# Local attention taken out of the recurrent chain and set among the gb projections, with ga projections in single contraction steps in its place

## The reference, cut to what matters

```python
proj = h @ w_in
aq, ak, av, bq, bk, bv, bz, ba, bb, ga, gb = jnp.split(proj, ...)
ya = swa_sink_attention(aq, ak, av, sink, rel_bias)     # 8 heads of 64, window of 128 keys, softmax with a sink
yb = gated_deltanet(bq, bk, bv, bz, ba, bb, ...)        # 4 heads of 128, chunkwise recurrence
merged = sigmoid(ga) * (ya @ w_up_a) + sigmoid(gb) * (yb @ w_up_b)
x = x + merged @ w_out
```

## Time and profile before

| | |
|---|---|
| time, median of 3 runs | 911.11 us (910.9 to 918.97) |
| the profiled execution: time, span | 917.6 us, 915.7 us |
| PE busy | 791.2 us, 86% of the span |
| DVE, ACT, POOL busy | 356.3, 244.5, 305.0 us |
| granted PE clock, mean | 0.942 |

### The profile page before, as it was taken

How to read it: one execution, slowest core, us unless ns; L and a number is a source line. 1 busy time by engine, 2 the same in 40 slices (tenths; PEclk the granted TensorE clock), 3 DMA queues, 4 the chain that set the end, 5 groups by cost and what they waited for, 6 DMA issues and landing times.

```text
span 915.7 us, 15044 instructions
## 1 busy us (share of the span) xinstructions
PE 791.2 (86%) x5907; PEld 659.2 (72%) x5907; DVE 356.3 (39%) x766; ACT 244.5 (27%) x421; POOL 305.0 (33%) x264
## 2 busy tenths in 40 slices
PE   5999999979988899998999898974999999887830
PEld 5888898868876788786799777863777767664620
DVE  6378750763567324233610712352111221111127
ACT  4333232431341234402222644330111111101003
POOL 3723344422250316213443344232333333322102
PEclk9999999999999889999999998976999999999985
DMA  9745504312021202464467273563999999999933
GB/s 252 132 96 102 115 2 92 65 29 46 1 47 47 47 1 48 96 188 97 96 189 161 47 230 132 213 242 136 390 392 387 395 388 387 382 385 391 369 137 162
DMA packets 73563, 162.88 MB, mean 178 GB/s; under 512 B 18876, under 2 KB 48396, under 8 KB 65320
## 3 DMA queue, kind: packets, MB, share of 16 engines
q1 hardware_dynamic: 65968, 150.66, 51.9%
q0 software_dynamic: 5696, 10.50, 3.3%
q10 hardware_dynamic: 1848, 1.02, 0.7%
HBM read 157.57 MB, written 13.04 MB: 186 GB/s over the span
## 4 chain that ended last, share of the span: by engine, by line
PE 63%; DMA 11%; DVE 11%; issue 7%; ACT 4%; POOL 2%; SPq 1%; DVEq 0%; POOLq 0%; ACTq 0%
PE bank L966 14%; PE bank L973 10%; PE bank L1295 10%; PE bank L974 10%; PE bank L975 10%; PE bank L1305 5%; DMA ring<-in_w_exp_down 4%; DMA arena<-in_w_exp_down 4%; PE bank L1282 2%; DMA ring<-in_w_cq 1%; DMA ring<-in_w_up_a 1%; DVE xres L1937 1%; PE bank L1316 1%; ACT w_high L1349 1%; DVE rt L1914 1%
## 5 line engine op out<-in xcount | busy, mean ns | idle before, releaser
L973 PE MATMUL bank<-h_hi,w_high 128*128 128x512 f32 x296 | 120.1, 406 | 0.0
L974 PE MATMUL bank<-h_lo,w_high 128*128 128x512 f32 x296 | 118.5, 400 | 0.0
L1295 PEld LDWEIGHTS bank<-arena,hT 128*64 128x64 f32 x1728 | 98.9, 138 | 24.7 <-issue 23.4
L789 POOL TENSOR_TENSOR ring_low<-ring,w_high 128x2048 fp32r<-128x2048 f32 (+1 forms) x16 | 72.3, 4522 | 114.3 <-ACT w_high L1349 114.1
L1295 PE MATMUL bank<-arena,hT 128*64 128x128 f32 x1728 | 102.5, 277 | 8.0 <-DMA arena<-in_w_exp_down 7.2
L789 POOL TENSOR_TENSOR w_low<-ring,w_high 128x2048 fp32r<-128x2048 f32 x14 | 64.4, 4598 | 80.8 <-ACT w_high L1349 80.7
L1910 DVE SCALAR_TENSOR_TENSOR rt<-rt,bank 128x128 f32<-128x128 f32 x32 | 9.2, 288 | 185.5 <-ACT rt L1550 185.5
L1349 ACT ACTIVATE w_high<-ring 128x2048 fp32r<-128x2048 f32 (+1 forms) x32 | 58.7, 1835 | 71.7 <-PE bank L975 25.7
L973 PE MATMUL bank<-w_high,h_hi 128*128 128x256 f32 (+1 forms) x208 | 63.9, 307 | 4.0 <-ACT w_high L1349 2.2
L975 PE MATMUL bank<-h_hi,ring_low 128*128 128x512 f32 x168 | 67.0, 399 | 0.0
L973 PEld LDWEIGHTS bank<-h_hi,w_high 128*128 128x128 f32 x296 | 56.7, 192 | 13.1 <-issue 0.3
(11 more groups left out here) (273 smaller groups left out, 1427.1 us busy)
## 6 DMA issues: line engine op xcount, KB each, us to landing
arena<-in_w_exp_gate SPq DMA_DIRECT2D x27, 1024.0 KB
arena<-in_w_exp_up SPq DMA_DIRECT2D x27, 1024.0 KB
arena<-in_w_exp_down SPq DMA_DIRECT2D x27, 1024.0 KB
ring<-in_w_in SPq DMA_DIRECT2D x33, 512.0 KB, 6.6
ring<-in_w_exp_gate SPq DMA_DIRECT2D x5, 1024.0 KB
ring<-in_w_exp_up SPq DMA_DIRECT2D x5, 1024.0 KB
ring<-in_w_exp_down SPq DMA_DIRECT2D x5, 1024.0 KB
xres<-in_x SPq DMA_DIRECT2D x8, 512.0 KB, 7.4
```

The source lines that it names most:

```text
L789: after(pool.tensor_tensor(low, full, high, ALU.subtract), w_lo)
L973: pe.matmul(o, l_hi, r_hi, start=(n == 0), stop=False)
L974: pe.matmul(o, l_hi, r_lo, start=False, stop=False)
L1295: ins = pe.matmul(bank[CAP * half:CAP * half + CAP, 1, P * n:P * n + P], xgT[:, x, kk, :], w[:, kk, P * half:P * half + P], start=(kk == 0 ...
```

## The change

- `sc`, `pt` and `pv` leave the chain. They stand behind it, among the eight gb jobs, with ty 0 to 3 in one place behind gb:2. The scores of even and odd tiles have a buffer each (in `xres`), and so have `stat` and `sums`.
- A ga job is cut into 8 contraction steps: seven new jobs `gp` and the last one, still called `ga`, all eight summed in one bank that is theirs alone while they last. The chain has the other 7 in turn. `pieces_after` says how many of them follow a job of the chain (0, 1 or 2).
- The output norm is made once for all four chunks, at gb:1, by DVE alone. The outputs of all four chunks are kept (`o_sb`), so no chunk waits for an earlier norm.
- The split weights use both halves of `w_high` in turn for all chunks, also those of the gates. The places at which POOL makes the softmax product are fixed (`SOFTMAX_AT`).
- The memory rows are loaded into `hT` and not into `rows`, after the last o2. The residual rows `x` are loaded again at the third up-projection chunk and not at the first.
- cv:0 and cv:1 are now halves of the columns, one chunk each, and not halves of the rows with two chunks each. The four ub of a half come ahead of the four ua. The split of yaT moves from gb:1 to cv:0, that of ybT stays at gb:4.

```diff
+def pieces_after(job):
+    k = job[0]
+    if k in ("tA", "tk", "tAT", "tv"):
+        return 1
+    if k in ("P", "PX") and job[1] % 2:
+        return 1 if job[2] < 5 else 2
+    return 2 if k in ("u", "S") or job == ("w", 1) else 0
...
-    for k, job in enumerate(delta):
+    pieces = [("gp", f, kk) if kk < KD - 1 else ("ga", f) for f in range(8) for kk in range(KD)]
+    for job in delta:
         jobs.append(job)
-        while n < len(other) and n * len(delta) < (k + AHEAD) * len(other):
-            jobs += other[n]
-            n += 1
-    jobs += [("gb", f) for f in range(3)] + [("ty", 2), ("ty", 3)] + [("gb", f) for f in range(3, 8)]
+        for _ in range(pieces_after(job)):
+            jobs += pieces[:1]
+            pieces = pieces[1:]
+    jobs += pieces
+    sc = [[("sc", t, 0), ("sc", t, 2), ("sc", t, 1), ("sc", t, 3)] for t in range(NT)]
+    pt = [[("pt", t, g) for g in range(4 if t else 2)] for t in range(NT)]
+    jobs += sc[0] + [("gb", 0)] + sc[1] + [("gb", 1), ("gb", 2)] + [("ty", c) for c in range(NT)] + pt[0] + sc[2] + [("gb", 3), ("pv", 0)]
+    jobs += pt[1] + sc[3] + [("gb", 4), ("pv", 1)] + pt[2] + [("gb", 5), ("pv", 2)] + pt[3] + [("gb", 6), ("pv", 3), ("gb", 7)]
...
-        jobs += [(k, f) for k in ("ua", "ub") for f in range(4 * half, 4 * half + 4)]
+        jobs += [(k, f) for k in ("ub", "ua") for f in range(4 * half, 4 * half + 4)]
...
-SOFTMAX_LEAD, NORM_LEAD = 3, 3
+SOFTMAX_AT = {("gb", 1): 0, ("sc", 2, 0): 1, ("sc", 3, 0): 2, ("gb", 5): 3}
...
     if k == "cv":
-        return [("cv", 0), ("cv", 256)]
+        return [("cv", 256 * job[1])]
...
+    for n, job in enumerate(jobs):
+        gates = at["gp", 0, 0] <= n <= at["ga", 7]
+        if job[0] in ("gp", "ga"):
+            bank_index[job] = BANKS - 1
+        else:
+            turn_no = (turn_no + 1) % (BANKS - 1 if gates else BANKS)
+            bank_index[job] = turn_no
...
+                if k in ("gp", "ga"):
+                    kk = job[2] if k == "gp" else KD - 1
+                    return split_sums(o, [(w_parts(c0, kk, P * (job[1] % 2), P), h_parts(kk))], KD, kk)
...
+                if job == ("gb", 1):
+                    job_empty(dve, ("o2", NT - 1))
+                    dve.wait_ge(zs_ready, 4)
...
+                    for ch, h in itertools.product(range(NT), range(B_HEADS)):
+                        n = 4 * ch + h
+                        ins = stt(out=zs[:, ch, h], in0=o_sb[ch][:, h], scalar=o_scale[:, n:n + 1], in1=zs[:, ch, h], op0=ALU.mult, op1=ALU.mult)
+                        mark(ins) if h < 3 else after(ins, y_ready)
```

More of the change, by code:

```diff
@@ L200, in emptied_by @@
 def emptied_by(job):
+    if job[0] == "gp":
+        return None
     return "act" if job[0] in ON_ACT or job[:2] == ("hT", "ffn") else "dve"
@@ L254, in program @@
                 xsum_count[summed] = count = count + 1
-    softmax_at = {jobs[at[("pt", t, 0)] - SOFTMAX_LEAD]: t for t in range(NT)}
-    norm_at = {jobs[at[("ty", c)] - NORM_LEAD]: c for c in (0, 2)}
     chunks, last_use = [], {}
@@ L281, in program, with before_part @@
         split_at[said.get(c) or first_use[split_chunks[m - 1]]] = m
-    high_of, before_in = [], []
-    for m, c in enumerate(split_chunks):
-        gate = c[0] == "w_in" and C_GA < c[1] <= C_GB
-        high_of.append(high_of[-1] if gate else 1 - high_of[-1] if m else 0)
-        earlier = [n for n in range(m) if high_of[n] == high_of[m]]
-        before_in.append(earlier[-1] if earlier else None)
-    assert high_of[part_of["w_in", C_GA]] == 1
+    def before_part(m):
+        return split_chunks[m - 2] if m >= 2 else None
+    bank_index, before_in_bank, held, turn_no = {}, {}, {}, 0
+    for n, job in enumerate(jobs):
[5 more added lines that the diff above has]
+            bank_index[job] = turn_no
+        before_in_bank[job] = held.get(bank_index[job])
+        held[bank_index[job]] = job
     bias_rows = nc.dram_tensor("bias_rows", (A_HEADS, WIN, BIAS_W), F32, kind="Internal").ap()
@@ L313, in program @@
         ids = sb("ids", [P, 2 * NT], I32)
[L314 removed]
+        TINY = 984
         tiny = sb("tiny", [P, TINY])
@@ L365, in program @@
         work["p"] = work["e"]
+        o_sb += [work["bgk"][:, b] for b in range(2)]
         ab_part = gate_a[:, 6, :]
@@ L577, in bank_of @@
         def bank_of(job):
-            return bank[:, at[job] % BANKS, :]
+            return bank[:, bank_index[job], :]
         def columns(tile, n, odd):
@@ L1200, in emit @@
                 if k == "cv":
-                    m = job[1]
                     job_empty(pe, ("hT", "mem", NM - 1, 1))
-                    for i, c in enumerate(chunks_of(job)):
-                        ins = sums(o[:, 256 * i:256 * i + 256], [(memT[:, kk, m * P:(m + 1) * P], wide(c)[:, kk, :]) for kk in range(KD)])
+                    for m in range(NM):
+                        ins = sums(o[:, 256 * m:256 * m + 256], [(memT[:, kk, m * P:(m + 1) * P], wide(c0)[:, kk, :]) for kk in range(KD)])
                     return ins
@@ L1267, in _ @@
             for n, job in enumerate(jobs):
-                if n >= BANKS:
-                    job_empty(pe, jobs[n - BANKS])
+                if before_in_bank[job] and before_in_bank[job][0] != "gp":
+                    job_empty(pe, before_in_bank[job])
                 if job[0] == "sc" and job[2] < 2:
@@ L1272, in _ @@
                 emit(job if job[0] != "sc" else ("sc", job[1], job[2] - 2)).then_inc(done, 1)
-            for job in jobs[-BANKS:]:
+            for job in held.values():
                 job_empty(pe, job)
@@ L1390, in norm_rows @@
                         job_done(act, ("hT", phase, t - 2, 1))
-                    after(nc.scalar.activation(rows[:, t % 2, :], source(t), ACT.Copy, scale=rstd[:, base + t:base + t + 1]), rows_ready)
+                    dst = rows[:, t % 2, :] if phase != "mem" else source(t)
+                    after(nc.scalar.activation(dst, source(t), ACT.Copy, scale=rstd[:, base + t:base + t + 1]), rows_ready)
                     if phase != "mem" and t >= 2:
@@ L1411, in _ @@
                     act.wait_ge(o_raw, c + 1)
-                    if c == 2:
-                        act.wait_ge(o_ready, 1)
                     for h in range(B_HEADS):
-                        n = 4 * (c % 2) + h
-                        after(nc.scalar.activation(oh4[:, h], o_sb[:, c % 2, h], ACT.Square, accum_out=o_stat[:, n:n + 1]), e if h == 3 else step["act"])
+                        n = 4 * c + h
+                        after(nc.scalar.activation(oh4[:, h], o_sb[c][:, h], ACT.Square, accum_out=o_stat[:, n:n + 1]), e if h == 3 else step["act"])
                 if k == "bias":
@@ L1818, in _ @@
                         rms(NORM_TILES["x"] + 2, 2, rstd_ready)
[L1819 to L1821 removed]
+                if job in (("gb", 4), ("cv", 0)):
+                    n, y = (0, yaT) if k == "cv" else (1, ybT)
+                    dve.wait_ge(h_hi_ready["y"], 2 - n)
                     after(tt(y_lo[:, 4 * n:4 * n + 4, :], y, y_hi[:, 4 * n:4 * n + 4, :].bitcast(F32), ALU.subtract), h_lo_ready["y"])
```

140 lines of the change are left out of this document (57 added, 83 removed).

## The result

The changed kernel takes 899.88 us (median of 4 runs, 899.58 to 899.97). The kernel before took 913.84 us (median of 4 runs, 910.9 to 918.97, the three shown above among them). The ratio is 0.9856, 95% interval 0.9815 to 0.9896. The change gains 14 us, about 1.5%. I had forecast 30 us and a time of 881, so it is faster, as the interval shows, but by less than half of what I said, and the time is outside my range (871 to 896).

The account below looks back on a forecast made before the run. PE was taken as the bound: 229 us = 190 work + 19 idle + 10 clock + about 10 left over. Gains of 25.5 and 5.2, about 30.5, gave 881 us from the median 911.11 (30 applied); range 871 to 896.

Parts of the forecast that it names:

- What bounds the kernel: PE from first G to last memory-row transpose: 229 us = 190 work, 19 idle, 10 clock, about 10 left over.
- 39 us beyond work: PE's idle, half-clock and leftover time in that stretch; 13.5 would be kept and 25.5 gained.
- changes of shape: PE switching between products of different shape: the leftover 10 us, some 40 changes before, about 12 after, 2.5 us kept.
- Part 2: Attention among the gb projections, output norm made once and hidden behind PE's work; gb stage about 75 us.
- pt 3 and pv 2: Gb stage, last softmax tile: pt 3 about 1.1 us late, pv 2 0.8, behind ACT and DVE work; sum 1.9.
- Part 1: Chain without sc, pt, pv and with ga by contraction steps: 7.4 us idle kept, chain about 128 us.
- for chunk b DVE ends some 0.2 us late: Inversion levels in the chain: PE waits 0.2 us for DVE in each of 8 levels, 1.6 us.
- Part 3: cv by column halves, ub ahead of ua: first chunk free 6.9 us earlier, wait and clock loss gone, gain 5.2 us.
- Rival 1: Attention becomes its own chain: each of four tiles delays pt or pv 2 to 3 us; 889 to 893; chance 0.18.
- Rival 4: Waits only move, since GpSimd's splits bound both; gain only 10 to 15 us: 898; chance 0.09.
- Rival 3: Chain recurrence paced by latency, not PE, so slower than before: 931 us; chance 0.05.
- Rival 2: Clock does not hold in the chain: 15 us lost instead of 1.7, 894 us; chance 0.10.

Follow-up runs that it names:

- e3: Changed kernel with the splits of the second and third gb weight chunks moved to o1:3 and pt 0,1: 894.17 us (0.9781).
- e1: Changed kernel with only the split of the second gb weight chunk moved, to o1:3 instead of gb:0: 896.11 us (0.9814).
- e5: Changed kernel with the split of ybT on ACT and DVE at gb:7 instead of gb:4: 904.58 us (0.991).
- e8: Changed kernel with the output norm's 16 DVE products given back to GpSimd as 8 operations: 899.75 us (0.9884).
- e9: Changed kernel with the ga pieces in the chain given out eight at a time, at the same mean rate: 924.31 us (1.0136).
- e11: Changed kernel with two weight splits and ybT split moved, attention one gate later, more setup pieces, memory-row norm at gb:6 instead of gb:5: 888.89 us (0.9742).
- e4: Changed kernel with cv:0 and cv:1 as row halves again, each reading both cv chunks: 905.08 us (0.9907).
- e12: e3 with four GpSimd products that nothing reads added behind the softmax product of tile 0: 899.94 us (0.9843).

## Why the prediction was wrong, step by step

**What bounds the kernel** held: the waits of the earlier trace rows and the falls of the clock beside them could be had. Of the 39 us beyond work I kept 13.5; the kernel kept about 30. One reading was short: a fourth stretch at half clock stands in the chain of before, behind a wait for L849, 3.4 us long (2 x 0.34 x 5):

```profile
270.00:275.00 5.00, 4.16 (x22) 3.79 (x22) 0.69 (x1) 0.46 (x1) 4.92 (x2) 0.66 0.00 0
```

So about 12 of the 39 us are clock, and 8 and not 10 were left for changes of shape; the sum stays.

**The step that failed is in Part 2**: the norm "ready at about 22.5 us after the chain's end, while PE reaches the last ty at 23.2: hidden, with under 1 us to spare". The norm was done after 30.4 us, 9.6 of them in the three meetings, and PE waited 5.1 us for it. In e3, where only the smallest meeting is left, it is done after 22.5; without that one it would be 20.8, an estimate from these numbers. So I had not counted DVE's own work too short (the 16 products take 4.7 us and not my 5.5), and what was missing is that these DVE operations, with both inputs in SBUF, do not run beside a GpSimd product here. The cover was short as well: in e3 PE starts the last ty 22.7 us after the chain's end, 1.4 us of that waiting in ty, and not at 23.2. So even there 1.1 us of waits for the norm is left. I had written that each microsecond beyond the cover is one of PE's, and had not asked which row speaks for a delay. The row at 346.11 did, and so did the mean of 909 ns of that line in the table of groups, beside 160 to 170 ns of its neighbours.

The gb stage, 12.6 us over my 75, in terms:

| term | forecast | measured |
|---|---|---|
| ty behind the norm | 0 | 5.1 |
| gb:2 behind its weights | 0 | 1.8 |
| pt 3 and pv 2 | 1.9 | 2.7 + 0.4 |
| clock | 0 | 14 us at half, some 2 of them idle: 6 |
| work and changes of shape | 73.1 | 87.6 less 10.0 and 6: 71.6 |

The gb:2 wait is a step that I left out: ACT's copy of that chunk stands behind the exponentials of tile 0, and GpSimd's difference starts only at 301.84. That is a queue and no meeting. One entry, in e1, took away this wait and the meeting at L1742. For pt 3 the queue that I counted was the right one, and 1.1 us became 2.7 because y_lo met a difference too: it started at 350.85 and lasted 4.31 us, for 2.29 in e5 where it meets none. The clock is the largest term that I had at nothing. I allowed one fall, for the chain; there was one, at 167.6. The three others stand beside the waits just named, so they are the price of the same errors. A wait of that size does not always bring one: in the profiled executions of e1 and e8 the same wait of 2.0 us stands at the start of the chain, and the clock is 1.00 from 157 to 172 us, where the changed kernel has 0.89. The work was, if anything, less than I said.

**Part 1**: 132.1 us for 128. The waits are 5.0 us, I had 7.4; the clock is as I said. The 6.5 that are left are mostly not idle in the profile. In one level of the inversion:

```profile
193.05 2.27 PE L969 MATMUL bank<-xres 128*128 128x128 f32 x16
```

Two P jobs by the earlier trace rows are 1.78 us; the second waits inside this group for DVE's transpose, which ends at 194.05. A level takes 5.3 us and not 4.9, eight times: 3 us. My "for chunk b DVE ends some 0.2 us late" was too small, the rest (about 3) I cannot place. That single contraction steps hold the chain together was right and undervalued: e9 gives them 23 us.

**How much of the miss is explained.** The time is 18.9 us above the forecast. e3, with two meetings and the gb:2 wait moved away, gives back 5.7, with new meetings in their place; e11, with other places besides and two pieces more in each setup, 11.0. About 8 are left. In e11's profiled execution the chain takes 129.8 us and the gb stage 77.3, together 4.1 over the forecast; for the rest no run here names the cause.

**Part 3** was right in mechanism and size: 5.0 for 5.2, and e4 gives back 5.2 us with the same wait.

**The rivals.** Rival 1, attention as a chain of its own with waits at each tile, is nearest in place and in kind, but its time, 889 to 893, was still too low; it named ACT's queue, and only 4.9 of the 10.0 us are of that kind. Rival 4 had the size (898) with a reason that is half right: "the waits only move, since something else bounds both (GpSimd's splits)". I dismissed it by GpSimd's busy share, which is no evidence when the question is at which moment it is busy. Rival 3's slower ending needs the coarse grain of e9. Rival 2 did not come in the chain.

**The median.** 911.11 was a low draw of the kernel before; 913.84 with one more run. It moves the forecast by 2 to 3 us and doesn't rescue it.

## What to carry to other kernels

When work is moved between DVE and GpSimd, or beside it, count their operations together wherever both read from SBUF, and lay the two timelines over each other before trusting "hidden". A margin under 1 us on a path with two engines and three queues is not a margin: price what its loss costs, the clock's fall included. A group whose mean is several times that of its neighbours of the same size can hide a wait that no view of waits shows, as the 909 ns did here. And moving one operation out of a meeting can put it into the next one, as in e3: lay the timelines over each other again after the move.

## What the runs showed of the hardware

A DVE operation with two inputs in SBUF (or a small TENSOR_SCALAR with one) that starts while a GpSimd product reads SBUF makes its pass only when that product is over: 0.17 us became 3.76, 1.83, 4.62 and, in e12, four times 1.13 to 1.16; in e3 2.02 and 2.60; 2.29 became 4.31. The held operation ends 0.02 to 0.03 us after the product where it is small, and one pass later (2.1 us) in the case of y_lo. The mask products of the chain, with one input in PSUM, keep their 0.69 us beside differences of 4.5 us, and so do DVE's transposes, with one input in SBUF, at 0.71 us (five of them beside a difference in the changed kernel). The Trainium skill states it (SBUF — State Buffer, section "Who interferes with whom"): a DVE instruction with two SBUF inputs contends with a GpSimd instruction that reads SBUF, the later one fully blocks, and one with at most one SBUF input does not contend unless it runs in a two-port mode, which a tensor_scalar can do. The trace agrees, for the fp32 operations with its numbers above; whether the held TENSOR_SCALAR of e12 (1.15 us for 0.17) ran in such a mode no run shows. My Part 2 did not use this rule, and names no GpSimd difference beside the norm.

It works in both directions. In the trace of before a y_lo on DVE and a difference on GpSimd overlap:

```profile
355.33 3.39 DVE L1822 TENSOR_TENSOR w_low<-arena,y_hi 128x2048 fp32r<-128x2048 f32 x1 [3.81 <-ACT y_hi L1349]
```

```profile
357.34 5.87 POOL L789 TENSOR_TENSOR ring_low<-ring,w_high 128x2048 fp32r<-128x2048 f32 x1 [0.76 <-ACT w_high L1349]
```

DVE's ends at 358.72, 1.38 us after GpSimd's start, and GpSimd's takes 1.3 more than its usual 4.5 to 4.6. One overlap seen in one trace, and no experiment, stands behind this direction.
